# A two-layer decoder trunk in one launch: x turned by the host, first weights laid out per chunk, constants packed

## The reference

```python
x = x + weight * rms_norm(fn(rms_norm(x, pre)), post)
def swiglu(h, wg, wu, wd):                 # D_MODEL 1024, D_FF 2816
    return (jax.nn.silu(h @ wg) * (h @ wu)) @ wd
```

## Time and profile before

| what | us |
|---|---|
| median of three runs (lowest, highest) | 970.74 (970.66, 970.95) |
| the profiled execution | 970.93 |
| its span, first to last instruction | 969.1 |

### The profile page before, as it was taken

One profiled execution on the slowest core, in us unless ns is written; L12 is line 12 of the kernel. 1 busy time (PEld: TensorE's weight loads), 2 busy tenths in 40 slices (PEclk: granted clock), 3 DMA queues, 4 the chain that ended last, 5 costly groups with the idle time before them and its releaser, 6 DMA issues.

```text
span 969.1 us, 13599 instructions
## 1 busy us (share of the span) xinstructions
PE 960.2 (99%) x4701; PEld 811.6 (84%) x4701; DVE 777.5 (80%) x1511; ACT 501.0 (52%) x813; POOL 128.1 (13%) x144
## 2 busy tenths in 40 slices
PE   8999999999999999999999999999999999999997
PEld 6888888899888888888888888888889888888886
DVE  6788988758669888888898878878779588888884
ACT  7434353678563534344645353466668465353432
POOL 5000000055610000000200000013242520000000
PEclk9999999999999999999999999999999999999999
DMA  9784747242674666567175747626750435656531
GB/s 308 248 279 157 257 163 260 82 143 88 189 237 161 201 212 215 175 207 237 55 271 167 256 147 243 217 88 199 263 179 18 152 109 201 233 193 197 200 104 43
DMA packets 126734, 178.12 MB, mean 184 GB/s; under 512 B 3258, under 2 KB 103700, under 8 KB 126688
## 3 DMA queue, kind: packets, MB, share of 16 engines
q1 hardware_dynamic: 122784, 170.63, 52.7%
q10 hardware_dynamic: 3088, 5.51, 1.8%
q0 software_dynamic: 816, 1.37, 0.5%
HBM read 176.41 MB, written 1.09 MB: 183 GB/s over the span
## 4 chain that ended last, share of the span: by engine, by line
PE 97%; DVE 1%; DMA 1%; ACT 0%; SPq 0%; issue 0%; DVEq 0%; POOLq 0%; POOL 0%; ACTq 0%
PE ps L1219 93%; PE ps L1473 1%; PE ps L1257 1%; DMA raw<-in_l_ffn_wu 1%; PE ps L1233 0%; PE ps L1611 0%; DVE w_lo L1749 0%; SPq L543 0%; DVE end_hi L2062 0%; PE ps L1330 0%; DVE down_lo L2053 0%; SPq L520 0%; DVE w_lo L1763 0%; ACT w_hi L846 0%; ACT logit L1016 0%
## 5 line engine op out<-in xcount | busy, mean ns | idle before, releaser
L1219 PE MATMUL ps<-w_hi,xt_hi 128*128 128x512 f32 (+3 forms) x912 | 354.0, 388 | 0.9 <-ACT w_hi L846 0.5
L1219 PE MATMUL ps<-w_lo,xt_hi 128*128 128x512 f32 (+3 forms) x912 | 351.3, 385 | 0.1
L1219 PE MATMUL ps<-w_hi,xt_lo 128*128 128x512 f32 (+3 forms) x912 | 351.3, 385 | 0.0
L1749 DVE TENSOR_TENSOR w_lo<-raw,w_hi 128x2048 fp32r<-128x2048 f32 (+3 forms) x107 | 234.6, 2232 | 49.8 <-ACT w_hi L830 49.4
L1841 DVE STREAM_TRANSPOSE ps<-h 32x128 f32<-32x128 f32 x624 | 201.4, 323 | 9.2
L830 ACT ACTIVATE w_hi<-raw 128x2048 fp32r<-128x2048 f32 (+3 forms) x110 | 200.0, 1865 | 6.8 <-DMA raw<-in_l_ffn_wu 4.1
L1219 PEld LDWEIGHTS ps<-w_hi,xt_hi 128*128 128x128 f32 x912 | 171.3, 188 | 33.9 <-DVE xt_lo L1778 0.8
L1219 PEld LDWEIGHTS ps<-w_lo,xt_hi 128*128 128x128 f32 x912 | 171.3, 188 | 33.6 <-DVE w_lo L1763 1.2
L1219 PEld LDWEIGHTS ps<-w_hi,xt_lo 128*128 128x128 f32 x912 | 171.2, 188 | 33.3
L934 ACT ACTIVATE ht_hi<-ps 128x512 fp32r<-128x512 f32 x40 | 24.0, 599 | 290.8 <-DVE ps L1841 286.8
L1219 PE MATMUL ps<-down_hi,ht_hi 128*128 128x512 f32 x320 | 124.9, 390 | 0.0
(11 more groups left out here) (235 smaller groups left out, 868.4 us busy)
## 6 DMA issues: line engine op xcount, KB each, us to landing
raw<-in_l_ffn_wg SPq DMA_DIRECT2D x42, 1024.0 KB, 7.3
raw<-in_l_ffn_wu SPq DMA_DIRECT2D x42, 1024.0 KB, 9.8
raw_down<-in_l_ffn_wd SPq DMA_DIRECT2D x40, 1024.0 KB, 5.0
raw<-in_l_w_in SPq DMA_DIRECT2D x5, 2048.0 KB, 7.9
raw<-in_l_w_out SPq DMA_DIRECT2D x4, 2048.0 KB, 7.8
xn<-in_l_ffn_wd SPq DMA_DIRECT2D x4, 1024.0 KB, 7.2
raw<-in_l_w_in SPq DMA_DIRECT2D x2, 1536.0 KB, 7.5
gpost<-in_l_ffn_post ACTq DMA_DIRECT2D x4, 512.0 KB, 5.8
```

The lines of the kernel that those rows point to most:

```text
L1219: return pe.matmul(dst, lhs, rhs, start=start, stop=stop, skip_group_check=True)
L1749: dve.tensor_tensor(part(w_lo), part(raw), part(w_hi).bitcast(F32), ALU.subtract).then_inc(main_lo, 1)
```

## The change

- The host lays out, for the first block, per partition and chunk, the turned x (256 columns) and the gate and up weights (512 columns) in one row, gains ahead of the first (`first`): one transfer per piece, with pieces of 1, 1, 1, 1, 2, 2 chunks. It lands in a new region that overlaps `bias` and the first ring buffer.
- `xt_hi` and `xt_lo` of the first stage are made from these rows in SBUF, 256 columns at once (VectorE makes the high part of the first two chunks, ScalarE the others). TensorE no longer turns x, gains or table there; `keep_busy` is 17 transposes once, in place of 8 and 6.
- The weights of the second and third block are packed too (`first_main`), one row per partition. The third block comes as two halves.
- The terms of the first two blocks alternate between the tiles. The second block goes to banks 7 and 3, and the last quarter of down(0), which writes bank 3, waits for the second block's multiply of tile 1 (`h_ready` 4).
- x in its own layout comes whole per tile, behind the first block's pieces. Small parameters are one packed array, the bias rows are laid out by the host (negated by VectorE), and both and `gpost` are loaded by SP behind the third block.

```diff
-    FIRST_PIECES = ((1, 1, 2, 2, 2), (2, 2, 2, 2))
-
-    WITH_MAIN = ((3, 4), (1, 3))
+    FIRST_PIECES = ((1, 1, 1, 1, 2, 2), (1, 1, 1, 1, 2, 2))
+
+    WITH_MAIN = ((4, 5), (3, 5))
...
+        first = lead[:, 2 * HEADS * SEQ + MAIN - KD - KD * (SEQ + 512):]
+        first_gain = first[:, 0:KD]
+        first_chunks = first[:, KD:].rearrange("p (k c) -> p k c", k=KD)
+        first_xt = first_chunks[:, :, 0:SEQ]
...
+        def gu_bank(u, jc, t):
+            return (7, 3)[t] if u == 0 and isinstance(jc, int) and jc == 1 else 4 + t
...
+            def first_main(i):
+                k, size = first_start(0, i), FIRST_PIECES[0][i]
+                cols = slice(0 if i == 0 else KD + k * (SEQ + 512), KD + (k + size) * (SEQ + 512))
+                sp.dma_start(first[:, cols], a["first"][:, cols]).then_inc(first_landed[0][i], 16)
+
+            def second_main(i):
+                k, size = first_start(1, i), FIRST_PIECES[1][i]
+                sp.dma_start(raw[:, 1, 512 * k:512 * (k + size)], a["first_main"][:, 0, 512 * k:512 * (k + size)])\
+                  .then_inc(first_landed[1][i], 16)
+
+            def third_main():
+                for i in range(2):
+                    cols = slice(i * MAIN // 2, (i + 1) * MAIN // 2)
+                    sp.dma_start(raw[:, 0, cols], a["first_main"][:, 1, cols]).then_inc(main_landed[0], 16)
+
+            def load_constants():
+                sp.dma_start(bias_rows, a["bias_rows"]).then_inc(rows_landed, 16)
+                sp.dma_start(small[:, :], a["small"]).then_inc(small_landed, 16)
+                sp.dma_start(gpost[:, :], bass.AP(tensor=a[f"{STAGES[0]}_post"].tensor, offset=0, ap=[[0, P], [1, D]]))\
+                  .then_inc(gpost_landed, 16)
+
+            def load_x(t):
+                sp.dma_start(x[:, t, :], a["x"][0, t * P:(t + 1) * P, :]).then_inc(x_landed[t], 16)
+
+            def first_blocks():
+
+                for i in range(len(FIRST_PIECES[0])):
+                    first_main(i)
+                load_x(0)
+                second_main(0)
+                second_main(1)
+                load_x(1)
+                for i in range(2, len(FIRST_PIECES[1])):
+                    second_main(i)
...
-                        ffn_main(s, j, n0 + j)
+                        if n0 + j > len(FIRST_PIECES):
+                            ffn_main(s, j, n0 + j)
+                        elif n0 + j == len(FIRST_PIECES):
+                            third_main()
+                            load_constants()
...
             def first_norm():
 
-                act.wait_ge(prep_done, 1)
-                turned_hi("norm0", 0, gain=0, groups=(0, 1))
-                split_first(0, 0)
-                split_first(0, 1)
-                turned_hi("norm0", 0, gain=0, groups=(2, 3))
-                turned_hi("norm0", 1, gain=0, groups=(0, 1))
-                split_first(0, 2)
-                turned_hi("norm0", 1, gain=0, groups=(2,))
-                split_first(0, 3)
-                turned_hi("norm0", 1, gain=0, groups=(3,))
-                split_first(0, 4)
+                for i in range(len(FIRST_PIECES[0])):
+                    act.wait_ge(first_landed[0][i], 16)
+                    for k in range(max(first_start(0, i), BY_DVE), first_start(0, i) + FIRST_PIECES[0][i]):
+                        act.activation(xt_hi[:, k, :], first_xt[:, k, :], ACT.Copy, scale=first_gain[:, k:k + 1])\
+                           .then_inc(first_x_hi, 1)
+                    split_first(0, i)
+                act.wait_ge(x_landed[0], 16)
                 x_squares(0, 0)
                 split_first(1, 0)
+                split_first(1, 1)
+                act.wait_ge(x_landed[1], 16)
+                x_squares(0, 1)
...
                 def first_step():
                     silu(0, 0, fixed)
-                    split_first(1, 1)
                     split_first(1, 2)
-                    x_squares(0, 1)
+                    silu(0, 1, fixed)
                     split_first(1, 3)
-                    silu(0, 1, fixed)
-                    load_gpost(STAGES[0])
+                    split_first(1, 4)
+                    split_first(1, 5)
...
+            def first_terms(n, chunks, tiles=range(TILES)):
+
+                for k in chunks:
+                    piece = [i for i in range(len(FIRST_PIECES[n])) if first_start(n, i) == k]
+                    for i in piece:
+                        with_main, count = first_count(n, i)
+                        pe.wait_ge((first_hi, main_hi)[with_main], count)
+                    if n == 0:
+                        x_is_high(pe, k)
+                    for t in tiles:
+                        mm(ps[:, gu_bank(0, n, t), :], xt_hi[:, k, t * P:(t + 1) * P], main_view(w_hi, n, k, 512), k == 0, False)
+                    if n == 0:
+                        pe.wait_ge(first_x_lo, k + 1)
+                    for t in tiles:
+                        mm(ps[:, gu_bank(0, n, t), :], xt_lo[:, k, t * P:(t + 1) * P], main_view(w_hi, n, k, 512), False, False)
+                    for i in piece:
+                        with_main, count = first_count(n, i)
+                        pe.wait_ge((first_lo, main_lo)[with_main], count)
+                    for t in tiles:
+                        ins = mm(ps[:, gu_bank(0, n, t), :], xt_hi[:, k, t * P:(t + 1) * P], main_view(w_lo, n, k, 512), False,
+                                 k == KD - 1)
+                        if k == KD - 1:
+                            ins.then_inc(gu_ready, 1)
...
+                            if u == 0 and isinstance(jc, int) and jc == 0 and (t, part) == (1, 1):
+                                pe.wait_ge(h_ready, 2 * 2)
...
+                def first_blocks():
+
+                    first_terms(0, range(0, 8))
+                    first_terms(1, range(0, 4))
+                    turn_first()
+                    first_terms(1, range(4, 8))
                 if u == 0:
-                    first_products()
+                    first_blocks()
                 else:
                     gate_up(0, fixed)
-                if aside:
-                    aside()
-
-                gate_up(1, fixed, between=turn_first if u == 0 else None)
+                    gate_up(1, fixed)
...
-            keep_busy(8)
-            pe.wait_ge(gains_landed, 16)
-            pe.transpose(ps[:, 3, 0:8], grows0, ident[0:8, 0:8]).then_inc(prep_ready, 1)
-
-            def turn_small():
-                pe.wait_ge(const_step, N_CONST)
-                pe.wait_ge(small_landed, 16 * N_SMALL)
-                pe.transpose(ps[:, 7, 0:G_ROWS], grows[:, :], ident[0:G_ROWS, 0:G_ROWS])
-                pe.transpose(ps[0:SLOTS, 7, P:P + BUCKETS], table[:, :], ident[0:BUCKETS, 0:BUCKETS])\
-                    .then_inc(prep_ready, 1)
-            ffn(0, 0, turn_small)
+            keep_busy(17)
+            ffn(0, 0)
...
+                dve.wait_ge(const_step, N_CONST)
+                dve.wait_ge(rows_landed, 16)
+                dve.tensor_scalar(bias_rows, bias_rows, -1.0, None, ALU.mult).then_inc(rows_step, 1)
+                dve.wait_ge(small_landed, 16)
+                dve.tensor_scalar(neg_sinks[:, :], sinks, -1.0, None, ALU.mult).then_inc(neg_sinks_ready, 1)
+            for i in range(len(FIRST_PIECES[0])):
+                for k in range(first_start(0, i), first_start(0, i) + FIRST_PIECES[0][i]):
+                    if k < BY_DVE:
+                        dve.wait_ge(first_landed[0][k], 16)
+                        dve.tensor_scalar(xt_hi[:, k, :], first_xt[:, k, :], first_gain[:, k:k + 1], None, ALU.mult)\
+                           .then_inc(first_x_dve, 1)
+                    x_is_high(dve, k)
+                    dve.scalar_tensor_tensor(xt_lo[:, k, :], first_xt[:, k, :], first_gain[:, k:k + 1],
+                                             xt_hi[:, k, :].bitcast(F32), ALU.mult, ALU.subtract).then_inc(first_x_lo, 1)
+                split_first(0, i)
             split_first(1, 0)
+            split_first(1, 1)
...
+    xt = np.asarray(inputs["x"])[0].T
+    gate, up = (chunks(np.asarray(inputs[f"l0_ffn1_{part}"])[:, 0:3 * FB]).reshape(P, KD, 3, FB) for part in ("wg", "wu"))
+    blocks = np.stack([gate, up], axis=3).transpose(0, 2, 1, 3, 4).reshape(P, 3, KD, 2 * FB)
+    lead = np.concatenate([chunks(xt), blocks[:, 0]], axis=2)
+    first = np.concatenate([columns(inputs["l0_ffn1_pre"]), lead.reshape(P, -1)], axis=1)
+    first_main = blocks[:, 1:].reshape(P, 2, MAIN)
...
```

More of the change, by code:

```diff
@@ L55 @@
 CROW = 32
+G_Q, G_KV, G_PEK, G_PEV, G_COLS = 48, 50, 51, 67, 83
+S_W2V = G_COLS
+S_W2K = S_W2V + 2 * HEAD
+S_ROPE = S_W2K + 4 * HEAD
+S_SINKS = S_ROPE + TILES * ROPE
+S_COLS = S_SINKS + HEADS
+ROW = SEQ + P
 FB = 256
@@ L78, in bucket_ranges @@
                      * np.float32(BUCKETS - exact)).astype(np.int32)
[L79 to L84, removed]
+    return np.where(n < exact, n, np.minimum(large, BUCKETS - 1))
 def trunk(nc, a, out):
@@ L217, in trunk @@
         cmp_ok = sb("cmp_ok", [P, TILES, CPAD])
```

(30 more changed lines are left out.)

131 lines of the change are left out of this document (47 added, 84 removed).

## The result

The change made the kernel slower: 973.30 us, median of 20 runs (971.30 to 974.89), against 970.88 us, median of 20 runs of the kernel before (970.38 to 971.33). The ratio is 1.0024, 95% interval 1.0017 to 1.0031: 2.4 us lost where 1.0 us of gain was forecast. The profiled execution took 973.34 us against 970.93, so it shows the same 2.4 us.

What follows compares the result with a forecast made beforehand. TensorE, busy in 99% of the span, was taken as the bound, so only the first 40 us count: 4.0 us gained at the launch less 3.2 waiting at bank 3, 0.8, stated as 1.0, gives 969.7 us; range 968.6 to 971.8.

Steps and rivals of the forecast that it cites:

- The launch: First block, up to the second block's start: it ends at 16.55 us, so down(0) can start 4.0 us earlier.
- the rate of the first transfers: Loads of the first blocks: 400 GB/s taken for rows of 3 to 8 KB, with 345 and 418 as ends.
- The second block's length: Second gate/up block: 48 products and four transposes stay at 11.52 us.
- the copies' costs: ScalarE's and VectorE's copies in the first block: about 0.42 us each for 256 columns, 1.23 for VectorE's 1024.
- The wait at bank 3: Before the last six products of down(0): TensorE waits 3.2 us, until VectorE's multiply frees the bank at 35.4 us.
- the slower rival: Third block's load lands late, at 32.2 us, and its products start at 40.4: 2.9 us lost, 973.6; chance 0.09.
- the free wait: Rival at down(0): the wait at bank 3 costs nothing and the kernel gains 4.0 us, 966.7; chance 0.05.
- granted clock 1.00 throughout, as before: Sign of being right, for the whole kernel: TensorE's granted clock stays at 1.00.
- the stated range: Whole kernel's time: from 968.6 us (a faster launch) to 971.8 us (a landing between two rivals), about 0.15 left out.
- the forecast of 1.0 us gained: Whole kernel: third block starts at 36.75 us instead of 37.53, stated as 1.0 us earlier, 969.7 us; chance 0.62.
- the 0.2 by which the forecast had been rounded up: At the third block's start: the net was 0.8 us, stated as 1.0 because one restart of TensorE's stream is gone.
- its last line: Signs of being wrong: no gap in down(0), a transfer releasing the third block's high parts, a shift changing after 40 us.

Runs made afterwards that it cites:

- e2: The kernel after with 25 transposes of the identity into the unused bank 4 ahead of the wait for bank 3: 971.23 us, ratio 1.0003 to the kernel before.
- e8: The kernel after with 12 transposes of the identity into the unused bank 4 ahead of the wait for bank 3: 971.13 us, ratio 1.0001 to the kernel before.
- e7: The kernel after run once more, nothing changed: 972.83 us, ratio 1.0020 to the kernel before.

## Why the prediction was wrong

**The launch came 1.0 to 1.2 us later than summed.** Chunk 0 landed at 4.2 (predicted 3.95), chunks 4 and 5 at 9.89 (8.86), their high and low parts were done at 11.7 and 13.0 (10.76 and 12.0), the second block started at 17.73 (16.55). The mis-sized term is the rate of the first transfers. 400 GB/s was taken from long rows in the middle of the kernel; the kernel after shows it only later:

```profile
3.00:4.00 1.00, 1.00 (x7) 1.00 (x6) 0.00 (x0) 0.00 (x0) 0.44 (x2) 1.00 0.96 361
4.00:5.00 1.00, 1.00 (x6) 1.00 (x6) 0.74 (x2) 0.63 (x1) 0.00 (x0) 1.00 0.97 338
5.00:7.50 2.50, 2.50 (x10) 2.08 (x9) 2.34 (x6) 1.46 (x3) 0.00 (x0) 1.00 1.01 365
7.50:10.00 2.50, 2.50 (x13) 2.07 (x12) 2.06 (x4) 1.34 (x4) 0.00 (x0) 1.00 1.00 387
12.50:15.00 2.50, 2.44 (x11) 1.67 (x10) 2.43 (x4) 2.50 (x5) 0.16 (x1) 1.00 1.05 415
20.00:22.50 2.50, 2.50 (x13) 2.07 (x12) 2.35 (x3) 1.49 (x2) 0.00 (x0) 1.00 1.03 419
```

Between the landings of chunk 0 (4.22) and of chunks 4 and 5 (9.89) lie 1.97 MB, so the pieces came at 1.97/5.67 = 347 GB/s where 400 was summed. The rows have some 370 in the same time; the rest would be later transfers that were already under way. At 400 these 1.97 MB take 4.9 us instead of 5.7; with the 0.3 us of chunk 0 that is the 1.0 us by which this landing was missed. The lower end of the range of rates, 345, was the right value, but not for the reason that the prediction tied it to, rows of 1 KB: these pieces have rows of 3 and 6 KB. (The prediction has all new rows at 3 to 8 KB; the single chunks of the second block have 2 KB.) The second block's length was right within 0.15 us (11.37 against 11.52), and the copies' costs were, too: ScalarE's two 256-column copies took 0.91 us and held it for 0.81 (0.84), the low part 1.23. The 1.2 us at the second block's start are 1.0 of the landing and 0.2 of small gaps in the chain of copies and products.

**The wait at bank 3 was right.** Its place, its releaser (the multiply on VectorE) and its length, 2.99 us against 3.2, came as predicted; the stretch from the high parts' start to the multiply's end is 36.28 - 29.45 = 6.83 us (6.84). ScalarE's high parts were released by the silu, not by a transfer: the third block, issued in two halves from 14.96 on, landed 12.2 us later (median of the two), by about 27.6, inside 26.6 to 28.6. So the slower rival as written, a late landing, did not occur, though its time, 973.6 us, is close to the one measured; neither did the free wait.

**The step that failed is "granted clock 1.00 throughout, as before".** The sum priced the idle time of TensorE by its length alone. By the runs, an idle time of 3.0 us in this place also halves the clock for about 3.4 us (37.5 to 40.9) soon after it. In the kernel after that is 0.26 us in the last products of down(0) and 1.33 us in the third block (+0.54 to +1.87), 1.6 us together, the same as the comparison with e2 gives. Without it, in e2 and e8, the time is 971.1 to 971.2 us: inside the stated range, but still no gain, and that part is the launch's mis-sized rate. A reader could have doubted this step: in the trace of before the longest idle time of TensorE behind the launch is 0.6 us, so that its clock of 1.00 said nothing about one of 3.

The Trainium skill, "TensorE: Matmul & The Clock Gate", section "HAM oscillation — how this bites in real kernels", describes this pattern: a wait for a transfer lets the clock drop, and the work behind the wait starts at the slow one. The trace agrees as to the two levels, 1.00 and 0.50; as to the moment it differs: the second to the fifth product behind the gap still start 0.23 us apart, and the clock falls 1.2 us after the work has come back (1.5 us in e7).

**The sum once more**, against the forecast of 1.0 us gained: the third block starts 1.3 us later than predicted (38.07 against 36.75), 0.9 of it from the launch and 0.4 from the six products behind the gap, which took 1.74 instead of 1.37 us; the half clock costs 1.3 more; 0.1 comes up to 649 us and 0.5 in the second mixer. With the 0.2 by which the forecast had been rounded up that is 3.4 us, the distance from -1.0 to +2.4. The second mixer's part was in no case of the prediction, and its last line was right in naming a shift that changes after 40 us as a sign of an error.

## What to carry to other kernels

A wait of some us in front of a saturated TensorE can cost more than its length, here 1.6 us more for 3.0: look for the granted clock behind it, in stretches of 0.5 to 1 us, since the busy share hides it, and where the wait can't be avoided try idle work in it (here twelve transposes of the identity were enough, for they left only 1.67 us idle). When a bank is reused sooner, follow who reads it last: here one silu and one multiply moved ahead of the next block's splits turned a loss of 2.4 us into a gain of 2.9. Pieces of a first transfer should be as small as the slowest of the engines that work on them needs, since two chunks in one cost 1.5 us at the second block's start and 1.1 in the time. And a landing that comes late costs nothing up to the spare time of what stands behind it (1.7 us in the second mixer): find the one wait that passes it on, as with `probt`, before the place of the data is blamed.

## What the runs showed of the hardware that was not expected

- The granted clock fell behind an idle time of 2.99 us, twice in two profiles, and not behind 1.67, 0.86, 0.39 or 0.26 us. It fell 1.2 and 1.5 us after TensorE had resumed, and stayed at half for some 3.4 us in both.
- In the kernel after the queues moved 338 to 387 GB/s from 3 to 10 us, mostly in rows of 3 to 6 KB, and 404 to 419 from 12.5 to 22.5 us. The Trainium skill, "DMA: Bandwidth & Descriptors", section Specifications, has about 358 GB/s as one core's share of a memory that two cores use; the 419 of this one core is well above it.
- The launch's first products started 0.50 us apart (5.13 to 6.13 for two) at a recorded clock of 1.00; in e2 they started 0.27 us apart (4.87 to 5.42 for two) at the same recorded clock. The slower start was covered by the later wait for chunks 4 and 5: down(0) starts at 29.10 in one and at 29.00 in the other.
